# First projections of a one-core inference step: three blocks of weight chunks become four blocks of channels

## The reference, cut to what matters

```python
mod = silu(cvec) @ w_ada + b_ada            # [2048] @ [2048, 6*2048], split in six
h = rmsnorm(x, g) * (1 + scale1) + shift1   # adaLN
p = h @ w_in + b_in                         # w_in [2048, 8192]
# columns of p: u_fourier 1024, q 1024, k 1024, v 1024, gate_A 2048, gate_B 2048
```

## Time and profile before

| | us |
|---|---|
| median of three runs | 1265.45 |
| profiled execution | 1263.68 |
| its span | 1261.9 |
| PE busy | 1156.0 (92%) |
| DVE busy | 511.2 (41%) |
| ACT busy | 373.8 (30%) |
| moved by DMA | 423.27 MB, mean 335 GB/s |

### The profile page before, as it was taken

The page is one execution under the profiler, slowest core; times in us unless marked ns, Lnnn a source line. Parts: engine busy times, 40 slices in busy tenths (PEclk is TensorE's granted clock), DMA queues, the critical chain, the costliest instruction groups (busy, mean ns, idle before and its releaser), DMA issues.

```text
span 1261.9 us, 14226 instructions
## 1 busy us (share of the span) xinstructions
PE 1156.0 (92%) x5577; PEld 685.2 (54%) x5577; DVE 511.2 (41%) x722; ACT 373.8 (30%) x530; POOL 44.3 (4%) x81
## 2 busy tenths in 40 slices
PE   5779899999999999999999999999798889888785
PEld 2236567766766676778887784444233324333232
DVE  0022445545533445546456646125133323323046
ACT  3222424433332333334445534221021111201013
POOL 0000210010000300000000000000000000000000
PEclk9689899999999999999999999999999999999998
DMA  9999999888774998886565558999999999999998
GB/s 379 407 376 354 323 327 360 289 315 286 280 268 161 327 320 310 319 281 206 179 249 185 174 193 345 421 422 419 422 421 421 421 421 421 421 421 420 421 408 322
DMA packets 105955, 423.27 MB, mean 335 GB/s; under 512 B 8865, under 2 KB 9041, under 8 KB 73121
## 3 DMA queue, kind: packets, MB, share of 16 engines
q1 hardware_dynamic: 101264, 410.55, 84.8%
q0 software_dynamic: 4032, 11.22, 2.9%
q10 hardware_dynamic: 592, 0.59, 0.1%
HBM read 418.37 MB, written 3.95 MB: 335 GB/s over the span
## 4 chain that ended last, share of the span: by engine, by line
PE 69%; DMA 27%; DVE 1%; ACT 1%; issue 1%; SPq 0%; DVEq 0%; POOL 0%; ACTq 0%
PE bank L719 14%; PE bank L721 13%; PE bank L720 13%; PE bank L1086 11%; DMA raw<-in_w_ada 8%; DMA mraw<-in_w_exp_up 6%; DMA mraw<-in_w_exp_gate 5%; PE bank L701 4%; DMA mraw<-in_w_exp_down 4%; PE bank L1116 3%; DMA mraw_g<-in_w_exp_up 2%; PE bank L1027 2%; PE bank L685 2%; DMA mraw_g<-in_w_exp_down 1%; PE bank L1157 1%; PE bank L865 1%
## 5 line engine op out<-in xcount | busy, mean ns | idle before, releaser
L1599 DVE TENSOR_TENSOR w_lo<-raw,w_hi 128x1024 fp32r<-128x1024 f32 x192 | 233.6, 1224 | 273.7 <-ACT w_hi L1257 273.2
L1257 ACT ACTIVATE w_hi<-raw 128x1024 fp32r<-128x1024 f32 x192 | 201.9, 1058 | 312.8 <-PE bank L721 221.4
L1086 PE MATMUL bank<-mraw,xg 128*64 128x512 f32 x904 | 233.5, 601 | 18.2 <-DMA mraw<-in_w_exp_gate 8.0
L719 PE MATMUL bank<-w_hi,h_hi 128*128 128x512 f32 x512 | 210.7, 411 | 3.9 <-DVE w_lo L1599 3.9
L721 PE MATMUL bank<-w_hi,h_lo 128*128 128x512 f32 x512 | 201.4, 393 | 0.0
L720 PE MATMUL bank<-w_lo,h_hi 128*128 128x512 f32 x512 | 201.4, 393 | 0.0
L1086 PEld LDWEIGHTS bank<-mraw,xg 128*64 128x64 f32 x904 | 73.5, 137 | 137.3 <-issue 133.4
L1116 PE MATMUL bank<-mraw,hidT 128*64 128x512 f32 x408 | 101.1, 596 | 24.2 <-DMA mraw<-in_w_exp_down 22.0
L719 PEld LDWEIGHTS bank<-w_hi,h_hi 128*128 128x128 f32 x512 | 97.3, 190 | 47.5 <-issue 29.2
L721 PEld LDWEIGHTS bank<-w_hi,h_lo 128*128 128x128 f32 x512 | 97.2, 190 | 21.5
L720 PEld LDWEIGHTS bank<-w_lo,h_hi 128*128 128x128 f32 x512 | 97.5, 190 | 19.5 <-issue 1.0
(11 more groups left out here) (260 smaller groups left out, 1140.7 us busy)
## 6 DMA issues: line engine op xcount, KB each, us to landing
raw<-in_w_in SPq DMA_DIRECT2D x64, 1024.0 KB, 5.8
raw<-in_w_ada SPq DMA_DIRECT2D x64, 1024.0 KB, 7.4
mraw<-in_w_exp_up SPq DMA_DIRECT2D x59, 1024.0 KB, 16.0
mraw<-in_w_exp_gate SPq DMA_DIRECT2D x58, 1024.0 KB, 16.0
mraw<-in_w_exp_down SPq DMA_DIRECT2D x51, 1024.0 KB, 16.0
raw<-in_w_ada SPq DMA_DIRECT2D x64, 512.0 KB, 7.9
raw<-in_w_out SPq DMA_DIRECT2D x16, 1024.0 KB, 5.0
raw<-in_w_na_o SPq DMA_DIRECT2D x8, 1024.0 KB, 5.4
```

What stands on the lines that cost most here:

```text
L719: nc.tensor.matmul(o, hi[:, k, s], wh, start=k == 0, stop=False)
L1086: last = nc.tensor.matmul(out[x * CAP:(x + 1) * CAP], xg[:, q * LOAD_K + kk, e * CAP:(e + 1) * CAP], slab(slot)[:, kk * COL:(kk + 1) * COL ...
L1257: nc.scalar.activation(w_hi[:, u % AHEAD], r, ACT.Copy).then_inc(hi_ready, 1)
L1599: v.tensor_tensor(w_lo[:, u % AHEAD], r, w_hi[:, u % AHEAD].bitcast(F32), ALU.subtract).then_inc(raw_done[n % RAW], 4)
```

## The change

- The first projections take four chunks (`P0_CHUNKS` = 4, so `L_MAIN` = 16) and go in four blocks of 512 channels (`BLOCKS` = 4). A block has 8 adaLN loads, one mod step, one fourth of h and one quad of each of the four chunks.
- These adaLN loads get a ring of their own, `araw`, with 4 slots of 1 MB in memory that is unused at that time, and a counter of their own (`ada_done`). Each is issued as two pieces whose rows are 512 columns (2 KB) instead of 1024 (4 KB): a load has 2 row tiles x 2 vectors x 512 columns.
- Chunks alternate between two pairs of banks from the start. What a quad gives can't stay in PSUM, so DVE adds it to `uqkv` after each quad (`add_partial`): 16 additions of two instructions instead of 4. PE waits for them before it uses a pair again (`banks_free`).
- h of stream 1 is formed by DVE itself (`modulate` on DVE), h of stream 0 by ACT. In blocks 1 to 3 DVE forms and splits the next h ahead of the additions of the block before.
- The mod step of the next block stands in the middle of the second unit of the third quad (`unit(l + 2, 1, b + 1)`).
- Five `ada_super` instead of nine lie before `L_MAIN`; the others stay one per dense load, so the last of them come 8 dense loads later. The places of the heads, of the mod steps and of the late work follow from the new `L_MAIN`.
- POOL loads four bias rows (instead of two) before it waits for all of h.

```diff
-        P0_CHUNKS = 3
+        P0_CHUNKS, BLOCKS = 4, 4
-        A_MAIN = A_SUPER + 7
+        A_MAIN = A_SUPER + 3
...
-                n = ADA_AT[16 * b + j]
-                slot_released(n)
+                n = 8 * b + j
+                if n >= ARAW:
+                    sp.wait_ge(ada_done, n - ARAW + 1)
                 for m in (SHIFT1, SCALE1):
-                    sp.dma_start(raw[:, n % RAW, 2 * m:2 * m + 2].rearrange("p (a k) n -> p a (k n)", a=1),
-                                 ada_v[:, j:j + 1, m * D + b * 2 * COL:m * D + (b + 1) * 2 * COL]).then_inc(raw_landed[n % RAW], 16)
+                    sp.dma_start(araw[:, n % ARAW, 2 * m:2 * m + 2],
+                                 ada_v[:, 2 * j:2 * j + 2, m * D + b * COL:m * D + (b + 1) * COL]).then_inc(part_landed[n % ARAW], 16)
...
+            for j in range(8):
                 ada_block_load(0, j)
+            dense_load(0)
+            for b in range(1, BLOCKS):
+                for ch, js in ((1, (0, 1, 2)), (2, (3, 4, 5)), (3, (6, 7))):
+                    for j in js:
+                        ada_block_load(b, j)
+                    dense_load(P0_CHUNKS * (b - 1) + ch)
+                dense_load(P0_CHUNKS * b)
+            for i in range(3):
+                ada_super_load(A_SUPER + i)
+                dense_load(L_MAIN - 3 + i)
...
+            for b in range(BLOCKS):            # PE
+                l = P0_CHUNKS * b
+                last_block = b == BLOCKS - 1
+                pe.wait_ge(h_ready, 2 * b + 2)
+                banks_free(l)
+                unit(l, 0)
+                next_ada(b + 1, (0,) if last_block else (0, 1))
+                unit(l, 1)
+                next_ada(b + 1, () if last_block else (2,))
+                banks_free(l + 1)
...
+                unit(l + 1, 0)
+                next_ada(b + 1, (1,) if last_block else (3, 4))
+                unit(l + 1, 1)
+                next_ada(b + 1, () if last_block else (5,))
+                banks_free(l + 2)
+                unit(l + 2, 0)
+                next_ada(b + 1, (2, 3) if last_block else (6, 7))
+                unit(l + 2, 1, None if last_block else b + 1)
+                banks_free(l + 3)
+                unit(l + 3, 0)
+                next_ada(b + 1, (4,) if last_block else ())
+                unit(l + 3, 1)
...
+            for b in range(BLOCKS):            # ACT
+                u = 2 * P0_CHUNKS * b
+                if b:
+                    high(u)
+                evac_block_rows(b)
+                if b:
+                    act.wait_ge(h_ready, 2 * b)
                 act.wait_ge(mod_ready, b + 1)
+                modulate(b)
+                if b:
+                    high(u + 1)
...
+            for b in range(BLOCKS):            # DVE
+                l = P0_CHUNKS * b
+                if b:
+                    low(2 * l)
                 mod_block(b)
+                modulate(b)
+                split_h(b, 1)
+                dve.wait_ge(htmp_ready, b + 1)
+                split_h(b, 0)
+                if b:
+                    add_partial(l - 2)
+                    low(2 * l + 1)
+                    add_partial(l - 1)
+                else:
+                    low(0)
+                    low(1)
+                for ch in range(1, P0_CHUNKS):
+                    low(2 * (l + ch))
+                    low(2 * (l + ch) + 1)
+                    if ch >= 2:
+                        add_partial(l + ch - 2)
```

More of the change, by code:

```diff
@@ L349, in landed_count, with ada_landed_count @@
         def landed_count(n):
-            return sum(32 if i in ADA_AT[:A_SUPER] else 16 for i in range(n % RAW, n + 1, RAW))
+            return 16 * (n // RAW) + 16
+        def ada_landed_count(n):
+            return 32 * (n // ARAW) + 32
+        ADA_PARTS = 32 * (A_SUPER // ARAW)
         ADA_LEAD = 2
@@ L703, in ada_super, with unit @@
                 last.then_inc(raw_done[n % RAW], 8)
-            def unit(l, half):
+            def unit(l, half, within=None):
                 chunk, quad, quads = chunk_of(l)
+                first, final = (LOAD_K * quad, LOAD_K * quad + 3) if l < L_MAIN else (0, LOAD_K * quads - 1)
                 n, u = DENSE_AT[l], 2 * l + half
@@ L787, in _ @@
[L787 to L798 removed]
+            for b in (6, 7):
+                pe.wait_ge(xT_ready, b - 5)
+                norm_transpose(x0, b, bank[b - 6])
@@ L1304, in _, with evac_block_rows @@
                                      ).then_inc(xT_ready, 1)
-            for b in range(2):
-                last = ADA_AT[16 * b + 15]
-                act.wait_ge(raw_done[last % RAW], 8 * (last // RAW) + 8)
+            def evac_block_rows(b):
+                act.wait_ge(ada_done, 8 * b + 8)
                 if b:
@@ L1637, in mod_block, with modulate @@
+            def modulate(b):
+                dve.wait_ge(xT_ready, 2 * b + 2)
+                dve.wait_ge(mod_ready, b + 1)
+                for j in range(4):
+                    k = 4 * b + j
+                    ins = v.tensor_scalar(htmp[:, 1, j], xT[:, k, 1], mod[:, 1, k, 1:2], mod[:, 0, k, 1:2],
+                                          ALU.mult, ALU.add)
+                chained(ins)
             def mod_block(b):
                 dve.wait_ge(modT_done, b + 1)
-                rows = bank[7 - b % 2][:, 0:32].rearrange("p (t m h s) -> p m h t s", t=4, m=2, h=2)
@@ L1641, in mod_block @@
-                for m in range(2):
-                    for half in range(2):
-                        ks = slice(8 * b + 4 * half, 8 * b + 4 * half + 4)
-                        ins = v.tensor_tensor(mod[:, m, ks], rows[:, m, half],
-                                              vecT[:, m, ks].unsqueeze(2).to_broadcast([P, 4, NS]), ALU.add)
-                chained(ins)
-                ks = slice(8 * b, 8 * b + 8)
+                ks = slice(4 * b, 4 * b + 4)
+                chained(v.tensor_tensor(mod[:, 0:2, ks], bank[7 - b % 2][:, 0:16].rearrange("p (k m s) -> p m k s", k=4, m=2),
+                                        vecT[:, 0:2, ks].unsqueeze(3).to_broadcast([P, 2, 4, NS]), ALU.add))
```

225 lines of the change are left out of this document (108 added, 117 removed).

## The result

| | before | after |
|---|---|---|
| median | 1264.74 us of 6 runs | 1258.99 us of 6 runs (1256.65 to 1259.73) |
| profiled execution, its span | 1263.68, 1261.9 | 1258.28, 1256.5 |
| PE, DVE, ACT busy | 1156.0, 511.2, 373.8 | 1157.2, 529.3, 368.3 |

The account below looks back on a forecast made before the run. PE was taken to bound 187.75 to 800 us, the start waiting on loads; the gain 194.1 - 178.1 = 16.0 took the profiled 1263.7 to 1247.7, median 1249.5. The range was 1238 to 1260 (the working's own 1245 to 1255).

Parts of the forecast that it names:

- first unit: Start of the first dense product on PE, after block 0's mod step and h: 40.5 us instead of 73.7.
- third load of block 0: Block 0's third dense load lands at 58.4; highs, low and addition add 4.5, so PE waits 5.0, until 62.9.
- first cycle: From PE's third load of one block to that of the next: 35.2 us, against 32.5 for 12 loads.
- last block: From the start of dense load 12 on PE to that of 16: 27.7 us of PE work, 1.0 for clock.
- T: The mark, start of unit 16 (dense load 16) on PE: 177.1, with low clock 178.1; gain 194.1 - T.
- rival A: 2 KB rows of the adaLN loads cost nothing, 2.56 us a load: gain 21, time 1244; chance 0.20.
- rival B: 2 KB rows in the start run at 348 GB/s, 3.01 us a load: gain 5.5, time 1260; chance 0.10.
- The end of the start: Up to unit 16: half clock after the 5.0 wait costs 2.8, 1.8 of it within the mod-step wait; T 178.1.
- wait for the copy: PE waits 1.8 per cycle at the mod step, as ACT copies sums only after the next block's first `high`.
- rival D: Low clock from each third-load wait to the next block's second adaLN load: +49, T 227, time 1298; chance 0.08.
- The term behind the mark: At unit 16, four dense loads (22.7) come before the mark, four adaLN loads (4.0) behind: 18.7 us less to do.
- Rival C: Bias loads and copy slow among dense loads, bias 16 us late at `add_mask`, PE idles as long: 1265; chance 0.10.

Follow-up runs that it names:

- first profile: Changed kernel without further edits, its first profiled execution: 1258.28 us, span 1256.5; median of the 6 runs of that set 1258.99 us.
- second profile: Changed kernel without further edits, profiled again beside the experiments: 1254.55 us, span 1252.7; median of 8 runs 1258.61 us, ratio to before 0.9965.
- copy first: ACT copies the adaLN sums ahead of the next block's first `high`, against the changed kernel: median 1252.77 us, ratio to before 0.9909.
- copy first, again: Second measurement of the changed kernel with ACT's copy ahead of the next block's first `high`: median 1256.60 us, ratio to before 0.9926.
- dummy products (one): Nine dummy matmuls fill PE's waits before the first unit and the third loads, against the changed kernel: median 1257.08 us, ratio to before 0.9929.
- either fix of the third load: Against the changed kernel: DVE's addition ahead of the two lows, 1264.53 us; or SP's third dense load ahead of the fifth adaLN load, 1259.84 us.
- one of the former together with it: Third dense load ahead of the fifth adaLN load and ACT's copy ahead of the first `high`, against the changed kernel: 1249.20 us, ratio to before 0.9882.

## Why the prediction was wrong in size

Its own steps, against the two profiles of after:

| step | predicted | first | second |
|---|---|---|---|
| first unit | 40.5 | 42.26 | 42.13 |
| third load of block 0 | 62.9 | 64.67 | 64.39 |
| first cycle | 35.2 | 38.93 | 36.33 |
| second cycle | 35.2 | 36.32 | 36.57 |
| third load of block 2 to unit 12 | 16.1 | 15.63 | 15.61 |
| last block | 28.7 | 30.07 | 28.75 |
| T | 178.1 | 185.62 | 181.65 |

Of the 16.0 forecast, the first profile lost 7.5 up to the mark, 1.9 in the term behind it and 1.2 in the rest; 5.4 are left, the difference of the two spans. The second lost 3.6, 1.9 and 1.3, and 9.2 are left. The rest is not explained.

**The loads were priced right.** The eighth load of 2 KB rows reaches PE at 32.63, where 31.42 + 8 x 0.15 gives 32.62, and 387 to 388 GB/s flow where loads follow each other without a gap. So rival A falls, and rival B (348) as well. The Trainium skill (page "DMA: Bandwidth & Descriptors", section Specifications) has line rate from 512 B up; the trace does not agree: 387 with 2 KB rows against 409 with 4 KB.

**The first unit** was 1.8 late for a small thing. After the last adaLN product ACT had to move out a transposed tile before it made the copy, which started at 35.31 instead of 33.7. This is the timeline of ACT in after:

```profile
34.82 0.60 ACT L1335 ACTIVATE xT<-bank 128x512 f32<-128x512 f32 x1 [2.11 <-PE bank L780]
35.31 0.59 ACT L1342 ACTIVATE modrow<-bank 128x512 f32<-128x512 f32 x1
```

**The failed step is the clock term in "The end of the start"**: "the wait of 5.0 should do the same and cost 2.8, of which 1.8 fall into the wait for the mod step. T = 178.1", +1.0 in all. Measured, in both profiles of after each cycle has a low stretch of its own; the cycle of 35.2 has no term for it. These two rows split the first cycle of the first profile at the first product of the next block's adaLN loads, at 86.0; the clock is low behind the third load and again behind the wait for the copy:

```profile
64.67:70.00 5.33, 5.33 (x20) 3.60 (x24) 0.09 (x1) 1.25 (x2) 0.54 (x1) 0.68 1.05 387
70.00:86.00 16.00, 15.00 (x68) 11.01 (x60) 12.97 (x22) 6.90 (x10) 0.54 (x1) 0.89 0.96 352
```

A cycle of 38.93 us at a mean clock of 0.90 has lost 3.9 us of full-clock work, one of 36.32 at 0.91 3.3; in the second profile 1.8 and 1.8 (0.95 twice). Taking the lost clock and the wait for the copy off each cycle leaves the last column:

| cycle | length | lost to clock | wait for copy | rest |
|---|---|---|---|---|
| after, first profile | 38.93, 36.32 | 3.9, 3.3 | 1.0, 0 | 34.0, 33.0 |
| after, second | 36.33, 36.57 | 1.8, 1.8 | 0.3, 1.2 | 34.2, 33.6 |
| copy first | 34.50, 33.49 | 0, 0 | 0, 0 | 34.5, 33.5 |
| copy first, again | 37.54, 36.07 | 1.9, 2.2 | 0, 0 | 35.6, 33.9 |
| dummy products (one) | 37.21, 36.09 | 1.9, 0 | 0.3, 1.2 | 35.0, 34.9 |

In the fourth row the mean clock of 0.92 gives 3.0, but 1.1 of that lies in the wait of 4.50, where it costs no work. The rest is 33.0 to 34.5 in the cycles of after and of the first execution with the copy first, and the prediction's own cycle without its wait for the mod step is 35.2 - 1.8 = 33.4 (its "32.3 of PE work" is a slip: 4 x 5.67 + 8 x 1.0 + 0.95 are 31.6, and nothing hangs on it). So its chain of work was right to about 1 us, and the two things added to it are not. I had priced the wait for the copy in full (1.8 per cycle) and low clock once; what is measured in after is low clock in each cycle and less of that wait. The account does not close everywhere: the first cycle of the fourth row is 1.1 us above the others, and with dummy products the rest is 34.9 to 35.0, so there full clock did not bring the cycle down to 33.4. That low clock lengthens a cycle is shown by two executions of one kernel and by this sum; the one edit that removed it does not confirm its size.

The reason why it adds to the cycle is one that the prediction had itself: PE's first adaLN product of a block releases the load on which PE waits 15 us later (16 to 19 us from that product to the next third load in these executions). From the third load to that product everything on PE is on the path, and the low stretches of after lie there. The two timelines of SP's queue show how the release carries over. In after that product starts at 86.0, 21.3 us behind the third load, and in the first execution with the copy first at 81.6, 17.2 behind it: the difference of 4.2 is about what the wait for the copy (1.0) and the clock of the two rows above (5.33 x 0.32 + 16.0 x 0.11 = 3.5) add up to. In after the three adaLN loads behind it (six pieces), one of which waits for that product, take until 89.6:

```profile
71.79 17.79 SPq L452 DMA_DIRECT2D araw<-in_w_ada  x6
89.62 0.47 SPq L476 DMA_DIRECT2D raw<-in_w_in  x1
```

and in the first execution with the copy first until 84.7:

```profile
70.38 14.28 SPq L452 DMA_DIRECT2D araw<-in_w_ada  x6
84.70 0.47 SPq L476 DMA_DIRECT2D raw<-in_w_in  x1
```

The dense load goes out 4.9 us earlier, and the third load of the next block starts 4.6 us earlier. (In the second execution with the copy first it goes out 1.4 us later than in the first, at 86.08, but the third load starts 3.2 later; 1.8 of that stays open.)

This also answers rival D: the direction of its mechanism was right (low clock behind the block's third load), its extent wrong: instead of 36 us per block, some 4 to 8 ran low (twice what was lost), and none in the first execution with the copy first.

**The term behind the mark** was 18.7 and is 16.8. Two windows of before give the prices in a stream of loads, four dense loads alone and four pairs of a dense and an adaLN load:

```profile
609.48:631.24 21.76, 21.76 (x98) 18.02 (x97) 11.00 (x10) 9.44 (x9) 0.00 (x0) 1.00 0.57 194
458.85:485.52 26.67, 26.67 (x130) 18.34 (x129) 11.01 (x10) 10.03 (x10) 0.56 (x1) 1.00 0.91 328
```

That is 5.44 and 6.67, so 1.23 for an adaLN load; 4 x (5.44 - 1.23) = 16.8. I had taken 5.67 and 1.0 from a place where an adaLN product stands beside a unit, and the difference of 0.23, one matmul step, belongs to the adaLN load. It counts four times on each side.

**The last block** is 1.4 over in the first profile and as forecast in the second. In after a load takes long to land there, with POOL's bias loads (q0) beside it, as the view of DMA queues and issues of 150 to 186 us shows:

```profile
q0 software_dynamic: 1072, 2.11, 20.3%
...
raw<-in_w_in SPq DMA_DIRECT2D x5, 1024.0 KB, 10.6
```

Rival C did not occur: PE has no wait at the first scores.

**What the range and the chances made of it.** The time lies in the range, near its upper end, where B had been put; it came there by another way, so that the range holds it is luck. The two scenarios with waits and clock (forecast and D) were kept as two, although between them lies the one that came, in which most waits cost a little clock.

## What to carry to other kernels

In a loop in which PE's progress releases the load that PE waits for later, count per turn all that delays PE between the two points, low clock included, and not idle time alone. Where two waits of one loop hide each other, an edit to one of them can show less than it is worth; here either fix of the third load brought nothing or harm, the fix of the other wait alone about 5 us, and one of the former together with it 9.4 (1258.61 to 1249.20, in one set of runs). Price work that is moved past a mark in the stream it is moved to, not from one place where it stands.
